# Two output tiles of a chunk summed side by side in every dense run of a two-block model

## The reference

```
first block, layer 0:  h = modulate(rmsnorm(x));  u = c*hv, 3-tap causal convolution, (b*conv) @ w_out
             layer 1:  RWKV-7 mixer: r, k, v = mixed inputs @ w_rkv, four small projections,
                       a scan over 512 steps per head (16 heads of 64), group norm, gate, @ w_o
             each:     x = x + gate1*mixer;  x = x + gate2*(relu(h @ mlp_w1)**2 @ mlp_w2)   (1024 -> 4096 -> 1024)
             end:      rmsnorm
second block, layer 0: gated delta rule: h @ w_in, 4-tap convolution, chunked recurrence, norm, @ w_out
             layer 1:  k, v = rmsnorm(h) @ w_kv;  k = rmsnorm(k per head) ; q = rmsnorm(hn @ w_q per head)
                       stick-breaking attention (8 heads of 128), @ w_out
             each:     h = h + mixer;  h = h + (silu(g)*u) @ w_down,  g, u = rmsnorm(h) @ w_gu   (1024 -> 2*2816 -> 1024)
```

## Time and profile before

| | before |
|---|---|
| median of 3 runs | 3384.2 us |
| the profiled execution | 3382.11 us, of it the span 3380.3 us |
| TensorE busy (matmul) | 2991.3 us, 88% |
| DVE busy | 1634.8 us, 48% |
| ACT busy | 1157.5 us, 34% |
| POOL busy | 201.9 us, 6% |
| chain that ended last | PE 77%, DVE 12%, ACT 8%, issue 1%, DMA 1%, POOL 1% |
| matmuls of lines 599, 601 and 606 | 2856 of each |

### The profile page before, as it was taken

One profiled execution on the slowest core, in us unless ns is written; L12 is line 12 of the kernel. 1 busy time (PEld: TensorE's weight loads), 2 busy tenths in 40 slices (PEclk: granted clock), 3 DMA queues, 4 the chain that ended last, 5 costly groups with the idle time before them and its releaser, 6 DMA issues.

```text
span 3380.3 us, 45348 instructions
## 1 busy us (share of the span) xinstructions
PE 2991.3 (88%) x20206; PEld 2436.6 (72%) x20206; DVE 1634.8 (48%) x2186; ACT 1157.5 (34%) x1506; POOL 201.9 (6%) x155
## 2 busy tenths in 40 slices
PE   3999999698999879999578888789999897799999
PEld 2887888476888768887366666567888785478887
DVE  5666553553677643232556565544333456443332
ACT  2225233342223134152443334323222456532221
POOL 1010000101222110001100000000000100010000
PEclk9999999899999989999789888899999998999999
DMA  6454543120000032222101001012232220022321
GB/s 226 183 196 149 199 175 114 50 87 34 3 3 3 3 125 100 100 97 90 50 25 38 26 25 38 13 38 77 81 115 82 96 76 24 1 100 84 110 87 68
DMA packets 41571, 269.70 MB, mean 80 GB/s; under 512 B 4256, under 2 KB 4512, under 8 KB 13344
## 3 DMA queue, kind: packets, MB, share of 16 engines
q1 hardware_dynamic: 38976, 260.01, 21.7%
q10 hardware_dynamic: 2400, 6.78, 0.5%
HBM read 264.68 MB, written 2.10 MB: 79 GB/s over the span
## 4 chain that ended last, share of the span: by engine, by line
PE 77%; DVE 12%; ACT 8%; issue 1%; DMA 1%; POOL 1%; POOLq 0%; DVEq 0%; SPq 0%; ACTq 0%
PE ps L599 19%; PE ps L606 19%; PE ps L601 19%; PE ps L1934 2%; PE ps L2570 1%; PE ps L1566 1%; PE ps L944 1%; PE ps L1549 1%; PE ps L956 1%; PE ps L1560 1%; PE ps L962 1%; DVE WL L413 1%; POOL ACC L500 1%; DVE k L988 1%; PE ps L463 1%
## 5 line engine op out<-in xcount | busy, mean ns | idle before, releaser
L599 PE MATMUL ps<-HH,WH 128*128 128x512 f32 x1928 | 767.3, 398 | 57.6 <-ACT HH L575 41.0
L601 PE MATMUL ps<-HH,WL 128*128 128x512 f32 x1928 | 758.4, 393 | 0.0
L606 PE MATMUL ps<-HL,WH 128*128 128x512 f32 x1928 | 735.4, 393 | 2.4 <-DVE HL L556 1.7
L413 DVE TENSOR_TENSOR WL<-ST,WH 128x2048 fp32r<-128x2048 f32 (+2 forms) x259 | 470.9, 1820 | 285.3 <-ACT WH L405 285.2
L405 ACT ACTIVATE WH<-ST 128x2048 fp32r<-128x2048 f32 (+2 forms) x211 | 382.7, 1814 | 320.2 <-PE ps L606 300.1
L599 PEld LDWEIGHTS ps<-HH,WH 128*128 128x128 f32 x1928 | 367.3, 191 | 146.9 <-issue 69.2
L606 PEld LDWEIGHTS ps<-HL,WH 128*128 128x128 f32 x1928 | 366.2, 190 | 83.2 <-DVE HL L556 4.5
L601 PEld LDWEIGHTS ps<-HH,WL 128*128 128x128 f32 x1928 | 367.5, 191 | 78.6 <-issue 2.9
L599 PE MATMUL ps<-GH,WH 128*128 128x512 f32 x928 | 361.6, 390 | 0.0
L601 PE MATMUL ps<-GH,WL 128*128 128x512 f32 x928 | 361.0, 389 | 0.0
L606 PE MATMUL ps<-GL,WH 128*128 128x512 f32 x928 | 359.8, 389 | 0.0
(11 more groups left out here) (350 smaller groups left out, 4052.4 us busy)
## 6 DMA issues: line engine op xcount, KB each, us to landing
ST<-w_m SPq DMA_DIRECT2D x64, 1024.0 KB, 4.8
ST<-w_gu SPq DMA_DIRECT2D x44, 1024.0 KB, 4.8
ST<-w_ada SPq DMA_DIRECT2D x40, 1024.0 KB, 5.7
ST<-w_dn SPq DMA_DIRECT2D x32, 704.0 KB, 4.0
ST<-w_gin SPq DMA_DIRECT2D x16, 1024.0 KB, 4.9
ST<-w_cin SPq DMA_DIRECT2D x12, 1024.0 KB, 4.8
ST<-w_rkv SPq DMA_DIRECT2D x12, 1024.0 KB, 5.0
ST<-w_kv SPq DMA_DIRECT2D x8, 1024.0 KB, 4.8
```

The lines of the kernel that those rows point to most:

```text
L413: o = e.tensor_tensor(WL[:, j % 3, cut], ST[:, pos % 3, cut], WH[:, j % 3, cut].bitcast(F32), ALU.subtract)
L599: e.matmul(big.tile((tag, m))[:, :], wh[:, k, c0:c0 + P], H[:, k, :], start=(k == 0), stop=False)
L601: e.matmul(big.tile((tag, m))[:, :], wl[:, k, c0:c0 + P], H[:, k, :], start=False, stop=False)
L606: o = e.matmul(big.tile((tag, m))[:, :], wh[:, k, c0:c0 + P], L[:, k, :], start=False, stop=(k == kt - 1))
```

## The change

In `tensor_dense` the list of groups no longer depends on the chunk's number: both tiles of every chunk form one group.

```diff
@@ -589,7 +589,7 @@
                 wh, wl = halves(j)
                 e.wait_ge(*lo.at(j))
                 tiles = [(n * (c // P) + i, i * P) for i in range(c // P)]
-                for group in ([tiles] if n == 0 else [[t] for t in tiles]):
+                for group in [tiles]:
                     for m, _ in group:
                         e.wait_ge(*big.free((tag, m)))
                     for k in range(kt):
```

## The result

The changed kernel takes 3420.07 us (median of 5 runs, 3416.83 to 3420.9), the kernel before in the same set 3382.4 us (5 runs). The ratio is 1.0104, 95% interval 1.0091 to 1.0118. In a later set, with 21 runs of the kernel before, it was 1.0101 (1.0087 to 1.0115). Forecast were 3414 us within 3402 to 3426, and 29.7 us more than the profiled execution of before; that of after is 35.7 us longer (3417.86 against 3382.11).

A forecast was written before the change was run, and what follows sets the result against it. TensorE bounds it: a dense run costs its matmuls times their start distance. 16.5 + 8.0 + 4.7 + 0.5 = 29.7 us on 3382.11 gives 3411.8, stated as 3414; own range 3407 to 3424, with a rival 3402 to 3426.

The forecast's parts named there:

- Distance of the starts and banks: In dense runs, matmul starts stay equally far apart and PSUM banks are free in time; both costed at 0.
- The wait in kk and qq: TensorE's second norm at a chunk's end waits for ACT's square; 2.75 us at six places, 16.5 us.
- norm(7) moves: At the end of qq, behind the last stall, norm(7) just moves; no cost of its own added.
- The chain that stood once in the trace before: End of qq, tiles 6 and 7: norm, Ln, Exp, Square, square, norm; 3.60 us norm to norm, 2.58 idle.
- The clock in kk and qq: Each 2.58 us gap lowers TensorE's clock afterwards; 1.6 us at five places, 8.0 us.
- cycling through banks: Dense runs: changing bank every second matmul lets the clock fall, about 170 us, 3584 us; rival, chance 0.01.
- r to k and k to v: Before HH is overwritten, two tile copies stand instead of one; 0.26 us later, twice, 0.5 us.
- The run ends: Behind conv_out, wo, gout, so: POOL's two sums in a row delay the norm 1.18 us, four times, 4.7 us.

The follow-up runs named there:

- order_only: Changed kernel, but conv_out, wo, gout, so, kk and qq keep the old order; 3385.19 us, ratio 1.0000 to the kernel before.
- fill: Changed kernel plus ten unused matmuls between a chunk's two norms at five of six places in kk and qq; 3409.64 us, ratio 1.0069 to the kernel before.
- after: The changed kernel, both tiles of every chunk in one group, against the kernel before; 3420.07 us, ratio 1.0104.
- before_again: The kernel before, unchanged, in one more profiled execution; 3383.77 us.
- before_ends_filled: The kernel before plus unused matmuls where TensorE idles at five run ends, three ahead of the norm's ones-matmul and six behind; 3376.68 us, ratio 0.9980.
- residual_ends_filled: Kernel before with filled run ends, plus tiles side by side in conv_out, wo, gout and so, four matmuls ahead there; 3379.03 us, ratio 0.9988.

## Why the prediction was right

- **Distance of the starts and banks, 0.** Right: order_only, ratio 1.0000, and the dense runs that the table's last line names have their old length to 0.01 us.
- **The wait in kk and qq, 16.5 us.** Right in its mechanism, 1.5 us low in size: 3.61 us from norm to norm at all six places; with the clock held up (fill, which left one of the six places open) the stretch costs 18.0. kk has 8.5 of it (4.73 in its later chunks, 3.81 from its last matmul to qq), 2.85 a place against the 2.75 costed. At qq's end there is 0.9 more: norm(7) moves, as I wrote, but into the low clock, where it takes 2.07 us instead of 1.13. The chain that stood once in the trace before was the price of the six new ones, because the order of ACT's queue is the same.
- **The clock in kk and qq, 8.0 us.** Right: fill takes 8.1 us back, 1.5 at each of the five filled places and 0.45 at qq's end. The Trainium skill ("TensorE: Matmul & The Clock Gate", section "HAM oscillation — how this bites in real kernels") tells of a kernel in which a DMA wait between bursts of matmuls makes the next burst start at the low clock each time; the trace agrees for waits on another engine, 0.92 over the later chunks of kk in after, 1.00 in fill. What the Trainium skill ("TensorE: Matmul & The Clock Gate", section "A second HAM failure mode: psum-queue depth-cycling") tells of cycling through banks, which the prediction weighed, does not show here: 1.00 over up01 and gu01 in order_only.
- **r to k and k to v, 0.5 us.** Right: 0.44 to 0.50; the wait before k is 1.56 instead of 1.30.
- **The run ends, 4.7 us.** The mechanism and its size are right, 1.18 costed and 1.20 measured. What was mis-sized is the end as a whole: 8.2 us in after (8.7 again). The term left out is the clock. The prediction put it at nothing without a word: the low clock behind an end is there already, and I didn't ask whether it would grow; it lasts 3.3 us longer at conv_out, wo and gout (0.72 over 24 us, against 0.79), while so's, at 0.72 before and after, grew by the sum alone. That the clock makes up the difference is shown by the two filled versions: 1.20 an end.
- **The rest of 35.7 us.** kk and qq 26.0, run ends 8.2 and r to v 0.5 make 34.7. What remains is 1: ab to gout +3.3 (seen in the unchanged kernel too), dn01 to kk and down11 to ab +1.8 together, and some -4 in stages up to wo (the scan -1.8, down01 to r -0.9, conv_in -0.9, up00's later chunks -0.5), of which before_again, with nothing changed, shows -3. That the total is off by 6 us (35.7 against 29.7) is 1.5 in kk and qq, 3.5 at the run ends and 1 in this rest; that the rest came out near nothing is luck, its parts are 4 to 5 us each way.

What stays open is where a fall of the clock lands. dn01 to kk and down11 to ab, which are not changed, are each 0.8 to 1.0 us longer in after because the norm's ones-matmul takes 2.07 instead of 1.12 us (at down11's end 2.08 instead of 1.13) behind a wait of the same length. down11 to ab is so in before_ends_filled too, where the residual order is the old one, and is not in residual_ends_filled, where it is the new one; so it isn't that order as such. Nor is it shown what picks one of the two lengths of the gated delta stage.

## What to carry to other kernels

Side by side or one by one is free for matmuls whose operands are there; what it moves is the moment at which the first tile is complete. So look at what is issued between the tiles on the same queue, and at the other engines' queues behind it: a wait that had half a chunk of cover can close a loop over two engines. Price it from a place in the trace where that loop already stands uncovered, and add the low clock that gaps of 2.58 us brought with them here.

## What was not expected of the hardware

- Useless matmuls in a gap pay: 50 in kk and qq took 8.1 us off the stretch, 45 at five run ends took 11.5 us off those ends and 0.2% off the kernel before; at the first of them the gain was lost again to the next wait.
- The gated delta stage has two lengths, some 3 to 4 us apart, in executions of one and the same kernel (3.46 in before, 3.04 in after). A difference of that size between two profiles isn't the change's until a second execution shows it.
